# Products of zeros ahead of the input, and the step-size unit and first channel unit formed together, contraction tile by contraction tile

## The reference

```python
h = jnp.concatenate([meta, x], 1)                     # 528 x 1024
...
def ssd_retention_mixer(h, w_in, ...):                # h is rmsnorm(h, mix_norm)
    u = h @ w_in
    z, xbc, dt_raw, q, k, v, g = split_cols(u, ...)   # dt_raw: 16 columns
...
def ssd_group(z, xbc, dt_raw, conv_w, conv_b, dt_bias, a_log, d_skip, norm_g):
    xbc = jax.nn.silu(causal_dwconv(xbc, conv_w, conv_b))
    dt = jax.nn.softplus(dt_raw + dt_bias)            # step sizes, one per head
    ...
```

## Time and profile before

| | |
|---|---|
| median of three runs | 1756.56 us |
| the profiled execution, its own time | 1754.83 us |
| its span on the core | 1753.1 us |
| TensorE busy | 1734.1 us, 99% of the span |
| VectorE busy | 1165.7 us, 66% |
| ScalarE busy | 755.5 us, 43% |

### The profile page before, as it was taken

How to read it: one execution, slowest core, us unless ns; L and a number is a source line. 1 busy time by engine, 2 the same in 40 slices (tenths; PEclk the granted TensorE clock), 3 DMA queues, 4 the chain that set the end, 5 groups by cost and what they waited for, 6 DMA issues and landing times.

```text
span 1753.1 us, 34038 instructions
## 1 busy us (share of the span) xinstructions
PE 1734.1 (99%) x13394; PEld 1654.7 (94%) x13394; DVE 1165.7 (66%) x1693; ACT 755.5 (43%) x1049; POOL 7.9 (0%) x35
## 2 busy tenths in 40 slices
PE   8999999999999999999999999999999999999997
PEld 7999999999999999999999899999989999999886
DVE  7888766557456777784334777777865788888333
ACT  5455433224334232222223877777774422323222
POOL 0000000000000000000000000000000000000000
PEclk9999999999999999999999999999999999999999
DMA  4332332222132322223223222222222232223321
GB/s 166 117 94 78 95 110 73 73 72 72 61 96 84 90 89 88 92 93 100 89 79 103 76 76 77 76 75 76 73 73 85 85 95 91 89 96 97 100 99 64
DMA packets 42845, 154.17 MB, mean 88 GB/s; under 512 B 5120, under 2 KB 6144, under 8 KB 42128
## 3 DMA queue, kind: packets, MB, share of 16 engines
q1 hardware_dynamic: 41440, 146.49, 26.8%
q10 hardware_dynamic: 1328, 6.60, 1.0%
HBM read 146.62 MB, written 2.13 MB: 85 GB/s over the span
## 4 chain that ended last, share of the span: by engine, by line
PE 93%; DVE 4%; ACT 2%; issue 1%; DVEq 0%; DMA 0%; SPq 0%; ACTq 0%
PE gp L425 81%; PE small L617 2%; PE small L461 2%; PE small L538 1%; PE small L668 1%; PE small L506 1%; PE small L679 1%; DVE wlo L1238 1%; PE small L639 1%; PE small L425 0%; PE small L453 0%; PE small L635 0%; DVE spb L1726 0%; PE small L647 0%; DVE xcv L1280 0%
## 5 line engine op out<-in xcount | busy, mean ns | idle before, releaser
L425 PE MATMUL gp<-hn_hi,whi 128*128 128x264 f32 (+1 forms) x3200 | 658.4, 287 | 0.1
L425 PE MATMUL gp<-hn_hi,wlo 128*128 128x264 f32 (+1 forms) x3200 | 649.4, 284 | 0.0
L425 PE MATMUL gp<-hn_lo,whi 128*128 128x264 f32 (+1 forms) x3200 | 648.8, 284 | 0.0
L777 ACT ACTIVATE whi<-raw 128x1024 fp32r<-128x1024 f32 (+1 forms) x248 | 272.9, 1100 | 726.8 <-PE gp L425 726.2
L1238 DVE TENSOR_TENSOR wlo<-raw,whi 128x1024 fp32r<-128x1024 f32 (+1 forms) x248 | 316.2, 1275 | 335.3 <-ACT whi L777 335.2
L425 PEld LDWEIGHTS gp<-hn_hi,whi 128*128 128x128 f32 x3200 | 499.9, 189 | 3.8 <-DVE wlo L1238 0.9
L425 PEld LDWEIGHTS gp<-hn_lo,whi 128*128 128x128 f32 x3200 | 496.1, 188 | 0.0
L425 PEld LDWEIGHTS gp<-hn_hi,wlo 128*128 128x128 f32 x3200 | 495.4, 189 | 0.0
L425 PE MATMUL gp<-hid_hi,wlo 128*128 128x264 f32 (+1 forms) x528 | 141.0, 321 | 0.0
L425 PE MATMUL gp<-hid_hi,whi 128*128 128x264 f32 (+1 forms) x528 | 140.9, 321 | 0.0
L425 PE MATMUL gp<-hid_lo,whi 128*128 128x264 f32 (+1 forms) x528 | 140.8, 321 | 0.0
(11 more groups left out here) (249 smaller groups left out, 1707.0 us busy)
## 6 DMA issues: line engine op xcount, KB each, us to landing
raw<-in SPq DMA_DIRECT2D x217, 512.0 KB, 3.5
raw<-in SPq DMA_DIRECT2D x32, 704.0 KB, 4.0
cs_bc<-cs_scratch ACTq DMA_DIRECT2D x4, 1056.0 KB, 5.8
q_turned<-qs SPq DMA_DIRECT2D x16, 132.0 KB, 4.1
k_turned<-ks SPq DMA_DIRECT2D x16, 132.0 KB, 4.0
out<-yT SPq DMA_DIRECT2D x8, 256.0 KB, 2.4
hT<-in SPq DMA_DIRECT2D x3, 528.0 KB, 6.3
rdec<-in ACTq DMA_DIRECT2D x1, 1056.0 KB, 6.4
```

The lines of the kernel that those rows point to most:

```text
L425: ins = pe.matmul(psum[:, h, 0:n_cols], wp[w.par][:, cols], rp[:, k0 + k, q0:q0 + n_cols], start=first and k == 0 and n == 0, stop=last an ...
L777: act.activation(whi[w.par][:, 0:kt * P], raw[w.par][:, 0:kt * P], ACT.Copy).then_inc(hi_done, 1)
```

## The change

Five edits, all at the beginning of the program.

1. VectorE zeroes `never2` first of all, and TensorE runs 20 products of it with itself (448 columns, bf16) into a PSUM bank that is written anew later. Their result is not used.
2. SP issues the block of unit 1 right behind `hT` tile 1, ahead of tiles 2 to 7.
3. ScalarE and VectorE split unit 1's block right behind unit 0's columns, ahead of tiles 2 to 7.
4. TensorE takes unit 0 and unit 1 together: for each contraction tile first unit 0's six products, then unit 1's six.
5. `sum_squares` stands behind the fourth contraction tile of unit 2, no longer behind its first.

```diff
@@ -111,6 +111,10 @@
 
 H_TILES = (slice(0, 1), slice(1, 2), slice(2, 4), slice(4, 6), slice(6, 8))
 H_FIRST = {t.start: c for c, t in enumerate(H_TILES)}
+
+
+
+ZEROS_AHEAD = 20
 
 
 class At:
@@ -279,7 +283,7 @@
         hi_done, lo_done, unit_done = sem("hi_done"), sem("lo_done"), sem("unit_done")
         hn_free = sem("hn_free")
         pair_free = [sem(f"pair_free{s}") for s in range(2)]
-        gain_in, vec_in, const_in = sem("gain_in"), sem("vec_in"), sem("const_in")
+        zeros_done, gain_in, vec_in, const_in = sem("zeros_done"), sem("gain_in"), sem("vec_in"), sem("const_in")
         h_in = [sem(f"h_in{c}") for c in range(KD // 2 + 1)]
         sq_done, acc_done, ssq_done, normln_done = (sem(n) for n in ("sq_done", "acc_done", "ssq_done", "normln_done"))
         rstd_done, nhi_done, nlo_done = sem("rstd_done"), sem("nhi_done"), sem("nlo_done")
@@ -332,9 +336,8 @@
 
             for c, tiles in enumerate(H_TILES):
                 sp.dma_start(hT[:, tiles, :], x_h[:, tiles, :]).then_inc(h_in[c], 16)
-                if c == 0:
-                    unit(At(0, 0, 0), w_dt[0])
-            unit(At(0, 0, 1), w_ssd[0])
+                if c < 2:
+                    unit(At(0, 0, c), (w_dt, w_ssd)[c][0])
             for c in range(1, 6):
                 unit(At(6, 0, W_SSD + c), w_ssd[c])
             with sp.Fori(1, SSD_GROUPS) as g:
@@ -462,16 +465,39 @@
                                         start=d == 0, stop=d == len(keys) - 1)
                 ins.then_inc(done, 1)
 
-            gemm(At(0, 0, W_DT), At(0, 0, T_DT), hn_hi, hn_lo, ready=(nlo_done, 0), psum=sp_[0:SSD_HEADS, 2:4, :],
-                 width=SSD_HEADS)
+            def zeros_ahead(n):
+
+                pe.wait_ge(zeros_done, 1)
+                for _ in range(n):
+                    pe.matmul(sp_[:, 0, 0:448], never2[:, 0:P], never2[:], start=True, stop=True)
+
+            zeros_ahead(ZEROS_AHEAD)
+            def first_units():
+
+                for k in range(KD):
+                    pe.wait_ge(nlo_done, k + 1)
+                    for unit, psum, width in ((0, sp_[0:SSD_HEADS, 2:4, :], SSD_HEADS), (1, gp[T_SSD % 2], P)):
+                        if k == 0:
+                            pe.wait_ge(lo_done, unit + 1)
+                            wait_count(pe, pair_free[(T_DT, T_SSD)[unit] % 2], (T_DT, T_SSD)[unit] // 2)
+                        cols = slice(k * P, k * P + width)
+                        for n, (wp, rp) in enumerate(((whi, hn_hi), (whi, hn_lo), (wlo, hn_hi))):
+                            for h in range(2):
+                                ins = pe.matmul(psum[:, h, 0:H2], wp[unit][:, cols], rp[:, k, h * H2:(h + 1) * H2],
+                                                start=k == 0 and n == 0, stop=k == KD - 1 and n == 2)
+                        if k == KD - 1:
+                            ins.then_inc(unit_done, 1)
+
+            first_units()
 
             def norm_first(k):
-                if k == 0:
+                if k == 3:
                     pe.wait_ge(const_in, 16)
                     sum_squares(0)
 
             for c in range(6):
-                hgemm(At(6, 0, W_SSD + c), At(6, 0, T_SSD + c), after=norm_first if c == 1 else None)
+                if c > 0:
+                    hgemm(At(6, 0, W_SSD + c), At(6, 0, T_SSD + c), after=norm_first if c == 1 else None)
                 if c == 3:
                     pe.wait_ge(cs_done, 1)
                     for n, src in enumerate((dtx, csr)):
@@ -808,9 +834,9 @@
                 if m == 1:
                     act.wait_ge(raw_in[0], 16)
                     act.activation(dt_cols(whi[0]), dt_cols(raw[0]), ACT.Copy).then_inc(hi_done, 1)
+                    split_hi(At(0, 0, 1))
             act.dma_start(cst[:], cst_h[:, 0:5 * P]).then_inc(const_in, 16)
             act.dma_start(vec[:, KD:NCOL], vec_h[:, KD:NCOL]).then_inc(vec_in, 16)
-            split_hi(At(0, 0, 1))
             for m in range(KD):
                 square(0, m, m % 2)
                 if m == 4:
@@ -1283,6 +1309,7 @@
                 ins.then_inc(done, 1)
 
 
+            ve.memset(never2[:], 0.0).then_inc(zeros_done, 1)
             for s in range(2):
                 ve.memset(ub[:, s, 0:3], 0.0)
             ve.memset(one_row, 1.0).then_inc(pair_free[0], 1)
@@ -1296,7 +1323,7 @@
                     ve.wait_ge(hi_done, 1)
                     ve.tensor_tensor(dt_cols(wlo[0]), dt_cols(raw[0]), dt_cols(whi[0]).bitcast(f32),
                                      ALU.subtract).then_inc(lo_done, 1)
-            split_lo(At(0, 0, 1))
+                    split_lo(At(0, 0, 1))
             for m in range(KD):
                 add_squares(0, m, m % 2, first=m == 0)
                 if m == 4:
@@ -1428,7 +1455,6 @@
                 ve.wait_ge(const_in, 16)
                 ve.tensor_copy(ident_b[:], ident)
                 ve.tensor_copy(never[:], cst[:, 4 * P:5 * P])
-                ch.link(ve.memset(never2[:], 0.0))
                 for at in (0, 272):
                     ve.tensor_copy(never2[:, at:at + P], cst[:, 4 * P:5 * P])
                 last = slice(5 * P - N_META, 5 * P)
```

## The result

The changed kernel takes 1759.61 us (median of 15 runs, 1757.82 to 1761.19); the kernel before 1755.94 us (15 runs, 1754.74 to 1756.92). The profiled execution took 1758.21 us, its span 1756.5 us, 3.4 us more than before.

The account below looks back on a forecast made before the run. TensorE, busy 99% of the span, was taken as the bound. -0.07 + 1.91 + 0.82 + 0.51 = +3.17 us on 1754.83 gave 1758.0; the middle between that and 1759.7 was forecast, 1758.8 us, range 1755.4 to 1761.3.

Parts of the forecast that it names:

- four waits: TensorE's new waits: 1.7 us for unit 1's split, 1.91 ahead of unit 2, 0.8 ahead of unit 3, 0.5 ahead of unit 5.
- The zeros: At the start, products of zeros raise TensorE's clock before the first real pairs, winning at most 1.75 us.
- The wait for unit 1's split: Behind three pairs TensorE idles 1.7 us until 10.01 us, giving back the clock's gain: -0.07 us.
- The wait for unit 0's buffers: Unit 2's split waits for unit 0's last product; TensorE idles 1.91 us, unit 2 starts at 22.89 us, 1.84 us later.
- The sum of squares: In unit 2, 4.02 us later; the delayed evacuation holds up unit 3 (+2.66 us in all), then unit 5 (+3.17 us).
- Sum: All steps at the beginning together: -0.07 + 1.91 + 0.82 + 0.51 = +3.17 us on 1754.83 us.
- Rival A: Clock falls back in TensorE's new gaps: +1.75 us per fall, 1759.8 to 1761.5 us for one; 15 in 100.
- Rival B: Start wins more, by a longer slow stretch or early landing of unit 1's block: 1755.8 to 1757.4 us; 15 in 100.
- C: Reusing unit 0's buffers costs nothing and the joint form wins 1.75 us or more: 1751 to 1754.5 us; 5 in 100.
- D: Zeros or earlier memset delay something held covered, or VectorE's lag outlasts 52 us: 1760 to 1763 us; 5 in 100.

Follow-up runs that it names:

- e1: The kernel before with the 20 products of zeros alone: 1755.04 us, ratio 0.9994 to the kernel before.
- e7: The changed kernel without any products of zeros, all else kept: 1761.10 us, ratio 1.0027 to the kernel before.
- e10: The kernel before with unit 1's block issued and split ahead of tiles 2 to 7, no zeros: 1756.19 us, ratio 0.9999 to the kernel before.
- e4: The changed kernel with own buffers for unit 0 and the sum of squares back behind tile 1 of unit 2: 1755.49 us, ratio 1.0001 to the kernel before.
- e8: The kernel before with only the sum of squares moved behind tile 4 of unit 2: 1757.65 us, ratio 1.0010 to the kernel before.
- e11: The changed kernel with the sum of squares behind tile 2 of unit 2 instead of tile 4: 1759.14 us, ratio 1.0021 to the kernel before.
- e5: The changed kernel measured again, unaltered: 1759.59 us, ratio 1.0020 to the kernel before.
- e12: The kernel before against itself, nothing changed: 1755.14 us, ratio 0.9995.
- e3: The changed kernel with more zeros: 27 ahead, 4 between first tiles of units 0 and 1, 8 between units 1 and 2: 1759.01 us.
- e6: The same kernel as e3, the changed kernel with its gaps filled with zeros, measured again: 1758.89 us, ratio 1.0017 to the kernel before.
- e2: The kernel before with the zeros and the sum of squares behind tile 2 of unit 2: 1754.49 us, ratio 0.9991 to the kernel before.

## Why the prediction was right

The forecast was 1758.8 us, "no change that can be told, though a slight loss", from new waits in four places. Measured: 1759.61 us, inside the range, with all four waits where they were forecast. The mechanism is right; that the number is so near is in part luck. The 1758.8 is the middle between 1758.0 and 1759.7 us, of which nothing in the trace chose one, and it stands on a median before of 1756.56 us (three runs), which came out as 1755.94 with fifteen. The loss in it is 2.2 us, and 3.67 were measured; the undivided +3.17 us was nearer.

- **The zeros.** End forecast near 6.9 us, measured 6.92. They cost nothing, and the slow stretch is gone; e1 and e7 show their worth as 1.1 and 1.6 us in the profiles.
- **The wait for unit 1's split.** Forecast end 10.01 us, measured 10.55; the sum of this step was -0.07 us and came out near +0.5. The term that was off is the landing of unit 1's block: 7.6 us forecast from one profile; ScalarE's split of it started at 8.19 us here, and at 7.63 to 9.03 us in the nine profiles with the early block. The forecast took the block's landing from that of tiles 2 and 3, which held its place before. ScalarE took those up at 7.70 us in that profile, the earliest of five with the order before (up to 8.70). An early tile 1 alone doesn't bring the block at 7.6: in e10 tile 1 was taken up at 5.71 us and the block at 8.03. Part of what looked like the change's loss in the two first profiles is this draw.
- **The wait for unit 0's buffers.** From unit 1's first pair to unit 2's: 22.89 - 10.01 = 12.88 us forecast, 12.91 measured; idle 1.91 against 1.75. e4 shows that the loss hangs on it.
- **The sum of squares.** 0.6 us to spare forecast; the last addition ended at 25.77 us and the sum started at 26.50, so 0.7. The wait ahead of unit 3 was 0.8 and is 0.75; from unit 3 to unit 5 it was 12.93 and is 12.80 us. e8 and e11 bear the mechanism out.
- **Sum.** +3.17 us forecast on the profiled execution, +3.4 in span, +3.67 in the medians. The near match hides two terms: unit 5 starts 3.84 us later instead of 3.17, mostly as the first wait ended late, and 0.5 us of it is won back before the end, which the forecast didn't have. The medians hold the falls of the clock besides.
- **Rival A** had 15 in 100 and turned out to be no alternative but a part: it comes on top in about two runs in five, by their granted clock, with 1.5 us where I had 1.75. The argument against it failed: the clock fell behind gaps of 2.78 and 0.76 us, both shorter than 3.94. e5's profile also shows what I had named as a sign of being wrong, pairs at 0.44 us behind 10 us. Rival A should have been weighed per execution, as a share of the runs.
- **Rival B** named a longer slow stretch or an early landing as a gain; the landing varies, but for both kernels alike, and the slow stretch of the kernel before is 4.4 us in e12 and 5.3 in e8 (edit 5 alone), not always 3.9. **C** is refuted by e4 and by the profile; **D** was not seen.

What stays open: what decides in which executions the clock falls; how much of the 3.7 us in the medians it makes, between the 0.6 to 0.7 us of e3 and e6 and the 0.9 us by which the changed kernel's runs without the lower clock are faster than its median; and whether e2's gain of 1.45 us over the kernel before would hold with more runs.

## What to carry to other kernels

When two units that take turns in double buffers are merged into one, the first of them holds its buffers until the end of both: look at which later unit needs them, and count its whole refill as uncovered (here the two splits, 1.1 and 1.2 us; the block itself had been loaded before). With buffers of its own for the small unit the merge costs nothing, but it won nothing here either (e4); the zeros alone did as well. What a faster clock wins can be taken again by the next wait (0.50 us ahead of the sum of squares in e1, none in e2 with the sum one tile later), so find that wait first. And take several profiles, of the start and of the end, before a half microsecond is put down to the order of transfers.

## What the runs showed of the hardware

- Products of zeros raise TensorE's clock: real pairs behind them at 0.24 instead of 0.44 us (the changed kernel, e1, e2).
- The clock can fall at gaps shorter than I had thought safe: 2.78 and 0.76 us of idle time with 0.7 us of work between them (e5). It did not fall in the first profile, with 1.95 and 0.79 us. The Trainium skill, page "TensorE: Matmul & The Clock Gate" (HAM oscillation — how this bites in real kernels), tells of a kernel in which waits for transfers of about 3 to 5 us brought the low clock back each time; here it came back behind shorter ones.
- At the end of the program it fell behind shorter idle times still, 0.67 and 0.57 us with eight one-column products between them. In five of fourteen profiles the last eight products then took 2.07 to 2.08 us instead of 1.16. In e5 the granted clock was 0.78 over the two microseconds in which they start and 0.50 over the next two.
- The slow stretch at the start lasted 3.9, 4.4 and 5.3 us in three profiles without a wait in it (before, e12, e8), and 9.3 us in one with a wait of 0.82 us (e10).
- The column of the granted clock stays at 1.00 in the slow stretch at the start, where the pairs are 0.44 us apart (before, e7, e10), and shows only a fall behind it (0.67 in e5). The spacing of equal products is the safer sign.
